# Key norms as one reciprocal per token and head, and the last two steps of a block inverse written by row ranges, in the RWKV heads of a two-block kernel

## The chip, the cores and the metric

One core of one Trainium2 chip runs the whole program: two transformer blocks over 512 tokens of width 1024. The metric is the device time of one execution in microseconds (µs); lower is better.

## The reference, cut to what matters

The change touches one stage of the second block, the RWKV-7 time mixing. For each of 16 heads of width 64, and each token, with r, k, v and the low-rank rates computed before:

```python
kk = heads(k * k_k)
kk = kk / jnp.maximum(jnp.sqrt(jnp.sum(kk * kk, axis=-1, keepdims=True)), 1e-12)
k = k * (1.0 + (a - 1.0) * k_a)
y = wkv7_scan(r_h, heads(decay), k_h, v_h, -kk, kk * a_h)
```

`kk` is divided by its own norm, which is one number per token and head. The scan is a recurrence over the tokens. The kernel does it in chunks of 128 tokens, and for each chunk and head it needs the inverse of a 128x128 unit lower triangular matrix, which it builds by doubling: blocks of 1, 2, 4, ... 64 rows, seven steps.

## The kernel before, in words

`rwkv_heads` (L1609) works on pairs of heads: 8 pairs, 128 channels each (two heads of 64) by 512 tokens (NCH = 4 chunks of 128). Each pair goes through four parts, and the loop `rwkv_turns` (L1577) runs them staggered, one turn for each pair:

- **invert** (pair i): steps s = 1 to 6 of the doubling (s = 0 is done by `grow_first`, L1798, without a product). In step s TensorE makes products of 64 columns in bf16 (`lx`, L2150), ScalarE casts them to a high part (`between`, L2003), VectorE writes the low part (`between_low`, L1813), TensorE multiplies again (`xlx`, L2168), ScalarE casts the high part into `added` (`added_high`, L2010), and VectorE writes the low part into `added` and copies both parts under a mask into the inverse X and its transpose XT (`grow`, L1821). The next step's `lx` of a head waits for that head's `grown`. Both heads go one after the other.
- **chain** (pair i-1): the recurrence over the 4 chunks in 12 parts, two in each step s, spread over TensorE, VectorE and ScalarE (L2181, L1838, L2017).
- **prepare** (pair i+1): early steps one by one in steps s = 1 to 6 (the tables `early`, L1781, L1979 and L2118), and the rest in `late`.
- **finish** (pair i-1): in `late`, at the end of a turn.

Every engine runs its own instructions strictly in the order in which the code writes them; semaphores tie the engines together (`steps.wait`, `steps.done`). So the order written in `turn` (L1921, L2074, L2241) is what decides. In step s VectorE does: `between_low`, the early step of prepare, the first part of the chain, `grow`, the second part of the chain. ScalarE does: `between`, the early step, chain, `added_high`, chain. TensorE does: `lx`, chain, `xlx`, chain, the early step.

The norm of the keys before: ScalarE squares kk in s = 2; TensorE multiplies it with a matrix of ones per head at the end of s = 3 (`norm`, L2109), which puts each norm's square on all 64 channels of its head; ScalarE takes the root of 128x512 in s = 4 (`root`, L1969), with a load of its table of functions before it; VectorE takes the maximum, the reciprocal and the product over 128x512 in s = 5 (`unit_keys`, L1753), and in s = 6 `keys_and_rates` (L1759). TensorE's step of s = 4 is `gate` (L2113), two products of 512 columns in f32 that another part of the head needs at the end of `late`; it writes bank 0 of PSUM, where the norm's product lay before.

At the end of a turn TensorE's `late` starts with the bonus product (L2122), then the transposes (L2128) and the products `grams` (L2147). VectorE's `late` starts with `columns` (L1765) and masks the grams as they come (L1789).

## Time and profile before

| | µs |
|---|---|
| median of 3 runs | 3725.72 (3723.64 to 3744.84) |
| profiled execution, its own time | 3741.53 |
| its span, from the first to the last instruction | 3739.7 |
| RWKV heads in it, from 1893 to 2568 | 675 |
| the eight turns start at | 1922.8, 1990.0, 2067.6, 2147.5, 2224.7, 2306.1, 2385.1, 2463.7 |
| TensorE busy over the span | 3078.2 (82%) |
| VectorE busy over the span | 2437.0 (65%) |
| ScalarE busy over the span | 1234.2 (33%) |

In the profile PE is TensorE (PEld its weight loads), DVE is VectorE, ACT is ScalarE. In a row of the timeline the first number is the start, in µs from the span's start, the second the duration of the piece, then engine, line, operation, written tile and read tiles, shape and count; in brackets the idle time of the engine before it and what ended it. Granted clock 1.00 is TensorE's 2.4 GHz level, 0.50 its 1.2 GHz level. The turn that starts at 2147.5 is used as the example; it is the fourth of the eight and has all four parts.

### The profile page before, as it was taken

To read this page: it belongs to the slowest core of one execution; us is meant where nothing else is said; L and a number is where in the kernel's file an instruction comes from. 1 tells how busy PE (TensorE), PEld (TensorE's weight loads), DVE (VectorE), ACT (ScalarE), POOL (GpSimd) and SP (SyncE) were. 2 spreads that over 40 slices of the span, in tenths; PEclk is the share of its full clock that TensorE was granted. 3 is DMA by queue.
4 is the path that set the end of the run, shared out by engine and by line. 5 is a ranking of instruction groups with operands and counts; after the bars stand their busy time and mean duration, and the time that the engine had idled before them with its cause. 6 is when DMAs were issued, how large, how long until landed. Compare 5 with 4: busy or idle time off the path is not lost. (4 is left out here: it accounts for less than half of the span.)

```text
span 3739.7 us, 59444 instructions
## 1 busy us (share of the span) xinstructions
PE 3078.2 (82%) x22778; PEld 1995.2 (53%) x22859; DVE 2437.0 (65%) x4209; ACT 1234.2 (33%) x1999; POOL 535.0 (14%) x365
## 2 busy tenths in 40 slices
PE   7686977459999999995967677775958998969987
PEld 4353444446766666663446566664445554434466
DVE  3893399967787877875357777764626553347742
ACT  2233132653333333333234334322114443223320
POOL 0550043013343333430000000000000000000000
PEclk9658988779999999997977777866955659979998
DMA  3003132478889898873100000002110006123230
GB/s 105 7 1 118 47 124 98 164 295 293 325 317 330 311 330 320 322 274 138 58 23 1 2 2 2 2 1 95 51 39 4 1 1 158 36 91 126 67 124 29
DMA packets 241977, 451.88 MB, mean 121 GB/s; under 512 B 15328, under 2 KB 153952, under 8 KB 240128
## 3 DMA queue, kind: packets, MB, share of 16 engines
q1 hardware_dynamic: 204928, 315.11, 24.1%
q0 software_dynamic: 36864, 134.23, 10.1%
q8 instruction: 124, 2.03, 0.2%
q14 instruction: 61, 0.50, 0.0%
HBM read 413.64 MB, written 35.65 MB: 120 GB/s over the span
## 5 line engine op out<-in xcount | busy, mean ns | idle before, releaser
L1310 PE MATMUL banks<-gated_hi,v_lo 128*128 128x384 bf16 (+2 forms) x1536 | 335.0, 273 | 0.0
L1310 PE MATMUL banks<-gated_lo,v_hi 128*128 128x384 bf16 (+2 forms) x1536 | 335.0, 273 | 0.0
L1310 PE MATMUL banks<-gated_hi,v_hi 128*128 128x384 bf16 (+2 forms) x1536 | 335.0, 273 | 0.0
L1297 PE MATMUL banks<-act_hi,u_hi 128*128 128x384 bf16 x768 | 252.2, 328 | 22.2 <-DVE u_lo L1232 22.2
L1297 PE MATMUL banks<-act_lo,u_hi 128*128 128x384 bf16 x768 | 252.2, 328 | 0.0
L1297 PE MATMUL banks<-act_hi,u_lo 128*128 128x384 bf16 x768 | 252.2, 328 | 0.0
L1143 POOL DMA_INDIRECT gathered_v<-in_v,first_tile_rows x128 | 177.9, 1390 | 499.5 <-DVE x_tokens L1246 470.5
L1138 POOL DMA_INDIRECT gathered_u<-in_u_rows,first_tile_rows x128 | 156.9, 1225 | 204.4 <-POOLq L982 146.7
L1310 PEld LDWEIGHTS banks<-gated_hi,v_hi 128*128 128x128 bf16 x1536 | 150.3, 98 | 55.4
L1246 DVE SCALAR_TENSOR_TENSOR x_tokens<-gathered_v,gathered_weights,x_tokens 128x1024 f32<-128x1024 f32 x128 | 164.2, 1283 | 10.4 <-DVE gathered_weights L1237 3.1
L1310 PEld LDWEIGHTS banks<-gated_hi,v_lo 128*128 128x128 bf16 x1536 | 139.5, 98 | 38.9
L1254 DVE CUSTOM_DVE_ANT_0 gathered_product<-gathered_u,first_tile_normed 128x1024 f32<-128x1024 f32 x128 | 155.9, 1218 | 3.3 <-DMA gathered_u<-in_u_rows,first_tile_rows 3.3
L1268 DVE TENSOR_TENSOR gated<-gelu,gate_group 128x384 f32<-128x384 f32 x96 | 53.4, 556 | 158.7 <-ACT gelu L1204 149.7
L1257 DVE TENSOR_TENSOR v_lo<-v_raw,v_hi 128x1024 bf16<-128x1024 f32 x128 | 156.1, 1220 | 0.0
L1204 ACT ACTIVATE gelu<-banks 128x384 f32<-128x384 f32 x96 | 47.1, 491 | 325.4 <-PE banks L1297 281.8
L1310 PEld LDWEIGHTS banks<-gated_lo,v_hi 128*128 128x128 bf16 x1536 | 139.5, 98 | 22.4
L1216 ACT CAST gated_hi<-gated 128x384 bf16<-128x384 f32 x128 | 65.2, 509 | 238.8 <-DVE gated L1268 227.2
L1232 DVE TENSOR_TENSOR u_lo<-u_raw,u_hi 128x1024 bf16<-128x1024 f32 x96 | 117.4, 1223 | 39.4 <-ACT u_hi L1189 39.3
L358 PE MATMUL banks<-act_lo,ffn_up_w_hi 128*128 128x512 bf16 x346 | 131.9, 381 | 12.7 <-DVE ffn_up_w_lo L317 12.4
L1196 ACT CAST v_hi<-v_raw 128x1024 bf16<-128x1024 f32 x128 | 133.4, 1043 | 0.0
L2008 ACT CAST between<-banks 128x512 bf16<-128x512 f32 (+1 forms) x96 | 52.8, 550 | 239.3 <-PE banks L2165 239.3
L358 PE MATMUL banks<-act_hi,ffn_up_w_hi 128*128 128x512 bf16 x345 | 131.3, 380 | 0.5
(608 smaller groups left out, 8281.2 us busy)
## 6 DMA issues: line engine op xcount, KB each, us to landing
v_raw<-in_v SPq DMA_DIRECT2D x128, 512.0 KB, 11.6
u_raw<-in_u SPq DMA_DIRECT2D x96, 512.0 KB, 11.7
gate_tables<-gate_piece SPq DMA_DIRECT2D x12, 2048.0 KB, 6.3
gate_group<-gate_tables SPq DMA_DIRECT2D x32, 768.0 KB, 15.8
ffn_up_raw<-in_ffn_up SPq DMA_DIRECT2D x20, 1024.0 KB, 7.3
early_u_raw<-in_u SPq DMA_DIRECT2D x32, 512.0 KB, 3.7
rwkv_in_raw<-in_w_in SPq DMA_DIRECT2D x5, 2048.0 KB, 7.9
ffn_down_raw<-in_ffn_down SPq DMA_DIRECT2D x3, 2816.0 KB, 14.5
```

The lines of the kernel that those rows point to most:

```text
L358: m = pe.matmul(bank[0:cols.stop - cols.start, :], w[:, slot, d, cols], x[:, d, :], **flags)
L1138: pool.indirect_dma_start(gu[:, n % GROUP, :], None, u_table, bass.IndirectOffsetOnAxis(ap=rows.index[:, 0, n:n + 1], axis=0)).then_inc(gu ...
L1143: pool.indirect_dma_start(gv[:, n % GROUP, :], None, v_table, bass.IndirectOffsetOnAxis(ap=rows.index[:, 1, n:n + 1], axis=0)).then_inc(gv ...
L1196: act.copy(vh[:, j, :], v_raw[:, j, :]).then_inc(v_hi, 1)
L1216: act.copy(wh[:, j, :], gh[:, j % 2, :]).then_inc(w_hi, 1)
L1232: dve.tensor_tensor(ul[:, j], u_raw[:, slot * LIVE + j], uh[:, j], ALU.subtract).then_inc(u_lo, 1)
L1246: dve.scalar_tensor_tensor(k.x[:, 0, :], gv[:, j, :], wts[:, slot, j:j + 1], k.x[:, 0, :], ALU.mult, ALU.add).then_inc(added, 1)
L1254: dve.tensor_tensor_reduce(prod[:], gu[:, j, :], rows.first[:], 1.0, 0.0, ALU.mult, ALU.add, dots[:, slot, j:j + 1]).then_inc(dotted, 1)
L1257: dve.tensor_tensor(vl[:, j, :], v_raw[:, j, :], vh[:, j, :], ALU.subtract).then_inc(v_lo, 1)
L1268: dve.tensor_tensor(gh[:, j % 2, :].rearrange("p (c t) -> p c t", t=TCH), src.rearrange("p (c t) -> p c t", t=TCH), gate[:, slot, :, j, :] ...
L1297: m = pe.matmul(ps[:, SCORE_BANK + (slot + j) % 2, 0:DT], u[:, j, d, :], x[:, d, P:], start=(d == 0 and n == 0), stop=(d == KD - 1 and n = ...
L1310: m = pe.matmul(ps[:, bank, to:to + width], v[:, j, cols], w[:, j, tok:tok + width], start=start and n == 0 and to == 0, stop=stop and n = ...
```

## The change

Two edits in the same function.

1. **Norms.** The square sums are made as 128 tokens x 2 heads for each chunk (kk squared is the stationary operand, two columns of the ones matrix the moving one), 8 numbers per partition in place of 512. Root, maximum and reciprocal work on 128x8. ScalarE then copies the reciprocals to 128x512 (`wide_norms`), and TensorE turns them back to channels with four products with the identity (`spread_norm`); VectorE multiplies kk with the bank. The steps move: maximum and reciprocal to s = 4, ahead of `key_rate`; the wide copy to s = 5, ahead of the decays; the spreading product to the end of s = 5; the product with kk to s = 6; and `gate` on TensorE from the end of s = 4 to the end of s = 6, since it waits for `unit`.
2. **Rows.** For s = 5 and 6 (blocks of 32 and 64 rows) `added` and the masked copies go. ScalarE casts the high part, and VectorE subtracts for the low part, straight into the row ranges of X and XT: in s = 5 four pieces of 32 partitions x 128 for each head and engine, in s = 6 one of 64 partitions x 256.

```diff
+BY_ROWS = 5
...
+        def rows_grown(slot, s, h):
+            b = 1 << s
+            for w, buf in ((0, X[:]), (1, XT2[slot])):
+                if s == STAGES - 1 and w == 0:
+                    continue
+                for n in range(HALF // b):
+                    first = (2 * n + 1 - w) * b
+                    rows = slice(first, first + b)
...
+                    yield bank, hi, lo
...
                 def unit_keys(j):
+                    steps.wait("prepare", "tensor", j, "spread")
+                    done(dve.tensor_tensor(kk, kk, ps[:, 0, :], ALU.mult), "unit", hold=True)
+
+                def inverse_norms(j):
                     steps.wait("prepare", "scalar", j, "root")
                     done(dve.tensor_scalar(nrm[:], nrm[:], 1e-12, None, ALU.max), hold=True)
-                    done(dve.reciprocal(nrm[:], nrm[:]), hold=True)
-                    done(dve.tensor_tensor(kk, kk, nrm[:], ALU.mult), hold=True)
+                    done(dve.reciprocal(nrm[:], nrm[:]), "inverse")
...
-                early = {1: square_root_argument, 3: decay_sums, 4: key_rate, 5: unit_keys, 6: keys_and_rates}
+                early = {1: square_root_argument, 3: decay_sums, 4: norms_and_rate, 6: keys_over_norms}
...
+                def grow_rows(i, slot, s):
+                    for h in range(2):
+                        steps.wait("invert", "scalar", i, f"added{s}{h}")
+                        for bank, hi, lo in rows_grown(slot, s, h):
+                            ins = dve.tensor_tensor(lo, bank, hi, ALU.subtract)
+                        steps.done("invert", ins, f"grown{s}{h}")
...
-                    done(act.activation(nrm[:], ps[:, 0, :], ACT.Sqrt), "root")
+                    done(act.activation(nrm[:], ps[:, 0, 0:2 * NCH], ACT.Sqrt), "root")
+
+                def wide_norms(j):
+                    steps.wait("prepare", "vector", j, "inverse")
+                    done(act.copy(nrm_wide[:].rearrange("p (n e) -> p n e", e=HD),
+                                  nrm[:].unsqueeze(2).to_broadcast([P, 2 * NCH, HD])), "wide")
...
-                early = {1: weights, 2: decay_in, 3: rate, 4: root, 5: decays}
+                early = {1: weights, 2: decay_in, 3: rate, 4: root, 5: norms_and_decays}
...
+                        if s >= BY_ROWS:
+                            for bank, hi, lo in rows_grown(slot, s, h):
+                                ins = act.copy(hi, bank)
+                            steps.done("invert", ins, f"added{s}{h}")
+                            continue
...
-                    done(pe.matmul(ps[:, 0, :], ones_h[:], kk2, start=True, stop=True), "norm")
+                    for c in range(NCH):
+                        ins = pe.matmul(ps[:, 0, 2 * c:2 * c + 2], kk2[:, c * P:(c + 1) * P], ones_h[:, 0:P:HD],
+                                        start=True, stop=True)
+                    done(ins, "norm")
+
+                def spread_norm(j):
+
+                    steps.wait("prepare", "scalar", j, "wide")
+                    for c in range(NCH):
+                        ins = pe.matmul(ps[:, 0, c * P:(c + 1) * P], nrm_wide[:, c * P:(c + 1) * P], k.ident[:],
+                                        start=True, stop=True)
+                    done(ins, "spread")
 
                 def gate(j):
-                    steps.wait("prepare", "scalar", j, "root")
+                    steps.wait("prepare", "vector", j, "unit")
                     pe.matmul(ps[:, 0, :], wj[:, 1, :], z[:, 25, :], start=True, stop=False)
                     done(pe.matmul(ps[:, 0, :], wj[0:32, 2, :], z[0:32, 26, :], start=False, stop=True), "gate")
 
-                early = {1: decay_in, 2: rate_in, 3: norm, 4: gate}
+                early = {1: decay_in, 2: rate_in, 3: norm, 5: spread_norm, 6: gate}
```

On TensorE, in the kernel before, step s = 4 of a full turn ends with the two gate products (L2115, L2116), between the chain's u product (L2202) and `lx` of step 5 (L2165):

```order
L2178 MATMUL banks<-between,inv 128x64 x12
L1574 REGISTER_ALU
L2202 MATMUL banks<-rhs,inv_t 128x64 x6
L1574 REGISTER_ALU
L2115 MATMUL banks<-z_columns,low_rank_w 128x512
L2116 MATMUL banks<-z_columns,low_rank_w 128x512
L1574 REGISTER_ALU
L2165 MATMUL banks<-inv,low_t 128x64 x12
```

In the changed kernel (its line numbers) the same two products (L2182, L2183) stand at the end of step s = 6, behind the last part of the chain (L2281 to L2283) and ahead of the bonus product (L2189) and the transposes (L2195):

```order
L2281 MATMUL banks<-state,r_dec 128x64
L2282 MATMUL banks<-u_tokens,grams_t 128x64
L2283 MATMUL banks<-bkv_tokens,grams_t 128x64
L1580 ISA
L2182 MATMUL banks<-z_columns,low_rank_w 128x512
L2183 MATMUL banks<-z_columns,low_rank_w 128x512
L1580 REGISTER_ALU
L2189 MATMUL banks<-rk,head_ones 128x512
L1580 REGISTER_ALU
L2195 MATMUL banks<-ident,b_dec 128x128 x4
```

So the gate has moved past two steps of the inverse and past six parts of the chain.

On VectorE, in the kernel before, step s = 5 of a full turn, from the norm (L1755 to L1757) to the first head's growth of the inverse (L1827):

```order
L1755 TENSOR_SCALAR kk_norm<-kk_norm 128x512
L1569 REGISTER_ALU
L1756 RECIPROCAL kk_norm<-kk_norm 128x512
L1569 REGISTER_ALU
L1757 TENSOR_TENSOR act_hi<-act_hi,kk_norm 128x512
L1569 REGISTER_ALU
L1574 REGISTER_ALU
L1851 TENSOR_TENSOR state_sum<-banks,state 128x64
L1569 REGISTER_ALU
L1852 TENSOR_SCALAR state<-state_sum,state_factors 128x64
L1574 REGISTER_ALU
L1827 TENSOR_TENSOR added<-banks,added 128x2x256
```

In the changed kernel step s = 5 has the state (L1893, L1894) at once and then the row ranges of both heads (L1858):

```order
L1850 TENSOR_TENSOR between<-banks,between 128x512
L1580 REGISTER_ALU
L1893 TENSOR_TENSOR state_sum<-banks,state 128x64
L1575 REGISTER_ALU
L1894 TENSOR_SCALAR state<-state_sum,state_factors 128x64
L1580 REGISTER_ALU
L1858 TENSOR_TENSOR inv<-banks,inv 32x4x32 x2
L1858 TENSOR_TENSOR x_tokens<-banks,x_tokens 32x4x32 x2
L1580 REGISTER_ALU
L1858 TENSOR_TENSOR inv<-banks,inv 32x4x32 x2
L1858 TENSOR_TENSOR x_tokens<-banks,x_tokens 32x4x32 x2
```

And in step s = 4 of the changed kernel the maximum and the reciprocal (L1780, L1781), which wait for ScalarE's root, stand ahead of the key rate (L1768 to L1771), and so ahead of the chain's right side (L1889, L1890), which follows:

```order
L1780 TENSOR_SCALAR kk_norm<-kk_norm 128x8
L1575 REGISTER_ALU
L1781 RECIPROCAL kk_norm<-kk_norm 128x8
L1580 REGISTER_ALU
L1768 ISA
L1768 TENSOR_SCALAR act_hi<-act_hi,cols,one_less 128x512
L1575 REGISTER_ALU
L1770 TENSOR_TENSOR act_hi<-act_hi,z_columns 128x512
L1575 REGISTER_ALU
L1771 ISA
L1771 SCALAR_TENSOR_TENSOR rk<-z_columns,cols,act_hi 128x512
```

The wait for the root, which stood in step 5, now stands in step 4, with all of VectorE's work of that step behind it.

## Rows read from the trace of the kernel before

**Rows 1.** Busy time by turn: the fourth turn, and the last, which prepares nothing

```profile
core 0: us, PE busy (x) PEld busy (x) DVE busy (x) ACT busy (x) POOL busy (x), PEclk, DMA share, GB/s
2147.50:2224.70 77.20, 57.04 (x764) 46.91 (x764) 61.22 (x128) 30.50 (x62) 0.00 (x0) 0.81 0.01 2
2463.70:2534.00 70.30, 50.72 (x660) 45.66 (x660) 41.85 (x90) 16.26 (x37) 0.00 (x0) 0.60 0.00 1
```

**Rows 2.** The fourth turn in three stretches, then step s = 5; columns as above

```profile
2147.50:2161.50 14.00, 8.15 (x112) 7.00 (x112) 8.35 (x18) 3.68 (x10) 0.00 (x0) 0.64 0.01 2
2161.50:2198.50 37.00, 28.65 (x489) 22.66 (x488) 31.13 (x62) 17.19 (x30) 0.00 (x0) 1.00 0.01 2
2198.50:2212.50 14.00, 12.47 (x91) 10.14 (x92) 10.36 (x23) 5.22 (x15) 0.00 (x0) 0.51 0.01 2
...
2188.20:2198.60 10.40, 6.88 (x125) 6.06 (x124) 9.19 (x15) 5.08 (x8) 0.00 (x0) 1.00 0.01 2
```

**Rows 3.** Timeline of the fourth turn, step s = 4 and the start of s = 5

```profile
2182.52 1.28 ACT L1971 ACT_TABLE_LOAD   x1
...
2183.15 0.54 DVE L1747 TENSOR_SCALAR act_hi<-act_hi,cols,one_less 128x512 f32<-128x512 f32 x1
...
2183.82 0.60 ACT L1971 ACTIVATE kk_norm<-banks 128x512 f32<-128x512 f32 x1
...
2185.26 0.28 DVE L1847 CAST rhs<-banks 128x128 bf16<-128x128 f32 x1
...
2185.93 0.35 PE L2202 MATMUL banks<-rhs,inv_t 128*128 128x64 bf16 x6 [1.19 <-DVE rhs L1848]
...
2186.11 1.10 PE L2115 MATMUL banks<-z_columns,low_rank_w 128*128 128x512 f32 x2
...
2188.20 0.52 PE L2165 MATMUL banks<-inv,low_t 128*128 128x64 bf16 x12
...
2189.79 0.52 PE L2165 MATMUL banks<-inv,low_t 128*128 128x64 bf16 x12 [0.72 <-DVE x_tokens L1834]
```

**Rows 4.** Timeline of the fourth turn, step s = 5 and the start of s = 6

```profile
2191.31 1.28 ACT L1975 ACT_TABLE_LOAD   x1
...
2192.38 3.35 DVE L1756 RECIPROCAL kk_norm<-kk_norm 128x512 f32<-128x512 f32 x1
...
2194.18 1.05 ACT L2015 CAST added<-banks 128x512 bf16<-128x512 f32 x2
...
2196.58 0.23 DVE L1851 TENSOR_TENSOR state_sum<-banks,state 128x64 f32<-128x64 f32 x1
...
2197.01 0.68 DVE L1827 TENSOR_TENSOR added<-banks,added 128x512 bf16<-128x512 f32 x1
2197.15 0.29 PEld L2195 LDWEIGHTS banks<-state,a_dec 64*128 64x128 f32 x2 [2.92 <-DVE state L1852]
...
2199.09 0.82 PE L2165 MATMUL banks<-x_tokens,low 128*128 128x64 bf16 x12 [0.41 <-DVE x_tokens L1834]
```

**Rows 5.** Timeline of the fourth turn, from the second head of s = 6 to the grams

```profile
2200.88 0.28 DVE L1847 CAST rhs<-banks 128x128 bf16<-128x128 f32 x1
...
2201.02 0.82 PE L2165 MATMUL banks<-x_tokens,low 128*128 128x64 bf16 x12 [1.11 <-DVE x_tokens L1834]
...
2206.70 2.02 PE L2122 MATMUL banks<-rk,head_ones 128*128 128x512 f32 x2
...
2208.51 1.06 PE L2128 MATMUL banks<-ident,b_dec 128*128 128x128 f32 x4
...
2212.89 0.73 DVE L1789 COPY_PREDICATED grams_t<-tri_masks,banks 128x512 f32<-128x512 uint32 x1 [3.12 <-issue]
```

**Rows 6.** Groups over the RWKV heads: prices of short VectorE and ScalarE operations

```profile
L1848 DVE TENSOR_TENSOR rhs<-banks,rhs 128x128 bf16<-128x128 f32 x31 | 9.0, 291 | 1.1
L1875 DVE RECIPROCAL gn_stats<-gn_stats 128x8 f32<-128x8 f32 x7 | 1.4, 195 | 0.3 <-ACT gn_stats L2041 0.3
L1950 ACT COPY low_rank_w<-decay_rate_w 128x128 f32 x6 | 1.8, 301 | 0.0
```

More of the change, by code:

```diff
@@ L1520, in rwkv_names, with held @@
     lows = [f"low{m}{h}" for m in range(2) for h in range(2)]
+    def held(s):
+        return ["-"] if s < BY_ROWS else []
     return {
         "prepare": {
-            "vector": ["kk", "-", "-", "sums", "-", "-", "rk", "-", "-", "-", "-", "-", "turnable", "-", "columns"]
+            "vector": ["kk", "-", "-", "sums", "-", "inverse", "-", "-", "rk", "unit", "-", "-", "turnable", "-", "columns"]
                       + grams[:4] + ["-"] + grams[4:] + ["bonus"] + ["-"] * 4,
-            "scalar": ["wj", "v", "decay_in", "kk2", "rate", "root", "-", "-", "decays", "-", "factors", "tok0", "tok1", "tok2",
+            "scalar": ["wj", "v", "decay_in", "kk2", "rate", "root", "wide", "-", "-", "decays", "-", "factors", "tok0", "tok1", "tok2",
                        *lows, "gate"],
-            "tensor": ["decay_in", "rate_in", "norm", "gate", "bonus", "turned0", "turned1", "turned2"] + grams + lows,
+            "tensor": ["decay_in", "rate_in", "norm", "spread", "gate", "bonus", "turned0", "turned1", "turned2"] + grams + lows,
         },
         "invert": {
-            "vector": ["-", "-", "-", "grown0"] + [n for s in stages for n in (f"between{s}0", f"between{s}1", "-", f"grown{s}0",
-                                                                         "-", f"grown{s}1")],
+            "vector": ["-", "-", "-", "grown0"] + [n for s in stages for n in (f"between{s}0", f"between{s}1", *held(s), f"grown{s}0",
+                                                                         *held(s), f"grown{s}1")],
             "scalar": [f"{n}{s}{h}" for s in stages for n in ("between", "added") for h in range(2)],
@@ L1638, in rwkv_heads @@
         x_room = k.x[:].rearrange("p t d -> p (t d)")
-        nrm = sb("kk_norm", [P, S])
+        nrm = sb("kk_norm", [P, 2 * NCH])
+        nrm_wide = sb("kk_norm_wide", [P, S])
         rk = sb("rk", [P, S])
@@ L1683, in view_blocks @@
             return buf.rearrange("p m (n two b) -> p m n two b", two=2, b=b)[:, :, :, odd, :]
+        def rows_grown(slot, s, h):
[6 more added lines that the diff above has]
+                    rows = slice(first, first + b)
+                    bank = ps[rows, 4 + h, :].rearrange("p (w m n b) -> p w m n b", w=2, m=NCH, b=b)[:, w, :, n, :]
+                    hi, lo = (buf[rows, h, l].rearrange("p m (n two b) -> p m n two b", two=2, b=b)[:, :, n, w, :]
+                              for l in range(2))
+                    yield bank, hi, lo
         def passes(left, right):
@@ L1819, in between_low @@
                                    f"between{s}{h}")
+                def grow_rows(i, slot, s):
[4 more added lines that the diff above has]
+                        steps.done("invert", ins, f"grown{s}{h}")
                 def grow(i, slot, s):
+                    if s >= BY_ROWS:
+                        return grow_rows(i, slot, s)
                     b = 1 << s
@@ L2084, in turn @@
                         if invert:
-                            added_high(i, s)
+                            added_high(i, slot, s)
                         if chained:
```

14 lines of the change are left out of this document (12 added, 2 removed).

## The prediction

> **What bounds the kernel now.** I read the busy time by turn first. The change lives in the RWKV heads, 675 µs of a span of 3739.7, and in them a full turn takes about 79 µs, of which TensorE is busy 57 and VectorE 61 [rows 1]. Neither is full, so the two take turns in waiting: a ring TensorE, ScalarE, VectorE, TensorE through each step of the inverse. Next the same turn in stretches [rows 2]. The granted clock is 1.00 from 2161.5 to 2198.5, through steps s = 2 to 5, and 0.51 from 2198.5 to 2212.5, just where TensorE is fullest (12.47 of 14.00). So TensorE runs its densest stretch at the 1.2 GHz level.
>
> Then the timeline of step 5 [rows 4] says why. VectorE holds everything: reciprocal from 2192.38 for 3.35, the state update only at 2196.58, growth of the inverse at 2197.01. TensorE waits 2.9 for the state and again for the inverse. It had been mostly idle for 4 µs when the clock fell. From 2201.02 on it has no wait worth naming until the grams; there VectorE waits 3.12 for it [rows 5]. So: VectorE bounds steps 4 and 5, TensorE bounds from step 6's second head to the grams. An edit is worth what it does to the bound of its own stretch. A program that differs by less than 1% (37 µs) is about what a measurement here can't tell from no change; over six full turns that is 6 µs a turn.
>
> All steps below are for the turn at 2147.5, as shifts against it.
>
> **Step 4, which gets longer.** VectorE now needs the root here. It is free at 2183.15; ScalarE's table load ends at 2183.80 [rows 3], and a root of 8 columns should take about 0.2 (the row of 128x8 on VectorE has 0.195 [rows 6]; both ends 0.15 to 0.3). So the root is there at 2184.0 and VectorE waits 0.9. Then maximum and reciprocal, 2 x 0.195 and a small gap: 0.45. Key rate, the chain's right side and the growth stand behind it, so all are +1.35. TensorE's u product, at 2185.93 behind VectorE's right side, comes at 2187.3.
> The gate leaves here: 2 x 1.10, from 2186.11 to 2188.2 [rows 3]. It was under cover: step 5's first product started at 2188.20 right behind it, and the second head's, at 2189.79, waited for VectorE 0.72. Both heads' growth comes 1.9 apart on VectorE, so the first was ready some 0.3 before its start: the gate's going gives that for one head and nothing for the other. First head +1.0, second +1.35.
>
> The Trainium skill (ScalarE: Activation LUTs, What ACT_TABLE_LOAD costs) says that a table switch takes about 2.66 µs, the load of 1.28 and a drain behind it of 1.38. If so, the root would come 1.4 later still and each full turn would lose that much more, some 8 µs in all. The trace does not agree: the load at 2182.52 ends at 2183.80 and the root starts at 2183.82 [rows 3]. I go by the trace.
>
> **Step 5, which gets shorter.** VectorE loses maximum, reciprocal and product, 2191.9 to 2196.58, 4.65 [rows 4]. What is late next? ScalarE. Its table load starts at 2191.31 and its first cast of `added` at 2194.18, 2.9 later, with the three exponentials between. Shifted by 1.35, and with the wide copy ahead (128x512, by the root's row 0.60 [rows 3]), the first cast starts at 2196.1. Then four pieces of 128 columns: 0.301 each alone [rows 6]; two casts of 512 take 1.05 where one takes 0.59, so neighbours overlap by about 0.1, and four take 0.9. VectorE's four pieces, 0.291 each [rows 6], with the same overlap take 0.95 behind it, the second head's another 0.95. Growth of both heads ends at 2198.9, where before it ended at 2200.88 [rows 5]. Gain 2.0 while TensorE is at its upper level. The row ranges bring 3.87 down to 1.9 of VectorE time; ScalarE pays 0.7 of it back.
>
> The Trainium skill (VectorE: DVE Perf Modes, The TRN2 errata) speaks against this edit: each instruction pays a fixed cost, so tile by 512 elements or more. Its figures would give a ScalarE cast of 128 columns from PSUM (172 + 128) / 1.2, an estimate of 0.25 without overlap, eight of them 2.0 against my 1.7: 0.3 more in a turn, 2 µs in all. The fixed part is in the trace too (128 columns cost 0.291, not a quarter of 0.68), but 0.95 for four pieces replaces 3.87 / 2 for a subtraction of 0.68 and two masked copies, so the edit still gains.
>
> The spreading product: 4 products of 128 columns, as many columns as one of 512, 1.1 at the upper level and 2.0 at the lower [rows 3, 5]. Bounds 0.5 (if short ones run like the transposes, 1.06 for four at the lower level [rows 5]) and 2.6. I take 1.0 and 1.9. In the upper case TensorE waits for the inverse anyway and it is hidden. The norm product in step 3 shrinks and was hidden.
>
> **The clock in steps 4 and 5.** TensorE finishes step 4's second multiplication at 2184.74 (1.19 idle before 2185.93 [rows 3]), then has the u product (0.35) at 2187.3 and nothing until 2189.2, since the gate that stood in this hole is gone. That hole is as empty as the one that let the clock fall before. I expect it to fall here, near 2191, and to return as it did before, 14 µs after [rows 2], near 2205. Then step 5 is bound by TensorE. A dozen products of 64 columns take 0.82 in place of 0.52 [rows 3, 4], 1.58 times as long. TensorE was busy 6.9 of step 5 at the upper level (the last of [rows 2]); that is 10.9 at the lower, and 1.9 for the spreading product makes 13, from 2189.2 on with small holes at the start. Step 6's first product starts near 2203, where it was 2199.09.
>
> **Step 6 and late.** From here on I take the upper level. The second head's first product of step 6 starts near 2204.6. From that point to the bonus product it took 5.7 at the lower level (2201.02 to 2206.70 [rows 5]); divided by 1.58 that is 3.6, to 2208.2. VectorE has added the product with kk, 0.7, and saved 1.4 in growth by rows, both beside TensorE's work: nothing. **The gate now stands on the path**: 2 x 1.10 to 2210.3 or so, bonus 1.1 to 2211.4, transposes start there, 2208.51 before [rows 5]: +2.9. Twelve transposes at 1.06 for four with some overlap take 2.7 at the lower level and half at the upper, 1.3 back, and the first grams, which began just before the clock's return, some 0.3. So +1.3 in each full turn; what follows (masks, the finish) hangs on the grams and moves along.
>
> **Sum.** Six full turns 6 x 1.3 = 7.8. The first two preparations (ahead of the loop, and in the first turn, without a chain) run at the lower level mostly: the gate, 4.0 there, becomes exposed, and what VectorE saves, about 1.4, goes off: 2.6 each, 5.2. The last full inverse (last turn, clock 0.60, and TensorE-bound): 0.5 gained by rows. +12.5. The profiled execution took 3741.53, 16 above the median of 3725.72; the sum is made on it, and I put the difference on the median: 3738, about 0.3% more.
>
> **Rivals.**
> *The clock stays up.* If the holes of step 4 don't drop it and step 5's hole is gone, step 6's second product starts at 2199.1 (2.0 before 2201.02), and the transposes at 2199.1 + 3.6 + 2.2 + 1.1 = 2206.0: -2.5, and -4.1 with what the transposes and grams give back. 6 x -4.1 + 4.7 = -20: 3706. For it: the reciprocal's hole, which let it fall before, is gone. Against: the new hole a step earlier. Chance 0.20.
> *The clock falls where it did before*, behind step 5 (holes in step 4 a little shorter than I think). Step 5 gains 2.0; then 2199.1 + 5.7 + 4.0, and the return near 2210 cuts the bonus to 1.5: transposes at 2210.3, +1.8, less 1.6 given back, +0.2. 6 x 0.2 + 4.7 = 6: 3732. Chance 0.22.
> *Slower.* The clock falls in step 4 and does not return before the gate, because step 5 still has holes. Then from 2204.6 there are 5.7 to the gate, 4.0 for it and 1.8 to the transposes, all at the lower level: 2216.1, 7.6 later than before. 6 x 7.6 + 4.7 = 50: 3776. It decides when the lower level lasts over 20 µs, as it does at the head of a turn, where TensorE has long holes. For it: the first rows of the turn stand at 0.64 [rows 2]. Against: at the lower level TensorE is full from 2192 on. Chance 0.10.
> The forecast has 0.43; 0.05 is left for what I don't see.
>
> **How the numbers follow.** The cases lie at 3706, 3732, 3738 and 3776; the runs before spread from 3724 to 3745. The range 3702 to 3762 holds the first three with some 6 µs for their sizes (root 0.15 to 0.3, spreading 0.5 to 2.6) and leaves out the slow one. Faster by over 1% (under 3688) would need the first rival doubled: 0.06. Slower by over 1% (over 3763): the slow rival, 0.09. Within 1%: 0.85.
>
> **What would show it.** Right: VectorE waits about 0.9 for the root in step 4 of each full turn; reciprocals of 0.2; TensorE's u product of step 4 starts 1.3 later after `lx` 4; the gate's two products run without a gap between the chain's last product and the bonus; the lower level begins in step 5, not 6. Wrong: a granted clock of 1.00 from step 2 to the grams (then the first rival), no wait for the root, or grams that come earlier in the turn than before.

## The result, and the profile after

| | kernel before | changed kernel |
|---|---|---|
| median (4 runs each) | 3724.68 (3719.05 to 3744.84) | 3755.94 (3753.77 to 3757.01) |
| ratio, 95% interval | | 1.0076 (1.0043 to 1.0109) |
| profiled execution, its own time | 3741.53 | 3755.15 |
| span | 3739.7 | 3753.4 |
| the same, measured more often | 3743.5 (26 runs, 3722.75 to 3759.53) | 3752.03 (10 runs, 3737.79 to 3758.82) |
| ratio of those | | 1.0028 (1.0008 to 1.0048) |

The change makes no difference above 1%. Four runs of a kernel can mislead here: before spreads over 37 µs in 26 runs, and three of its first four lay at the fast end, so the first two medians are 31 apart. Measured more often, the change costs 0.28%, some 10 µs. The forecast was +12.5.

The page of the changed kernel, the parts on busy time and on the granted clock in 40 slices (of about 94 µs each; the RWKV heads are slices 21 to 28):

```profile
span 3753.4 us, 59680 instructions
...
PE 3112.2 (83%) x22890; PEld 2032.0 (54%) x22971; DVE 2387.5 (64%) x4177; ACT 1243.4 (33%) x2055; POOL 533.9 (14%) x365
...
PEclk9658988679999999997977777776965559979998
```

VectorE lost 49.5 µs of work, TensorE gained 34.0. Of TensorE's gain 14.4 is the new spreading product; most of the rest is the same work at a lower clock, as the next rows show. The heads and their parts in the changed kernel: from the first memset to the next normalization (this ends some 9 µs behind the 2568 of the table of before), the six full turns, the end behind the last inverse, and the attention stage of the same block, whose code the change doesn't touch:

```profile
core 0: us, PE busy (x) PEld busy (x) DVE busy (x) ACT busy (x) POOL busy (x), PEclk, DMA share, GB/s
1896.30:2581.30 685.00, 519.71 (x6224) 437.65 (x6224) 443.26 (x986) 254.77 (x552) 5.49 (x4) 0.71 0.02 8
1998.40:2473.80 475.40, 378.48 (x4668) 322.78 (x4668) 330.74 (x740) 192.80 (x416) 0.00 (x0) 0.73 0.01 2
2473.80:2581.30 107.50, 73.84 (x792) 63.87 (x792) 48.33 (x109) 20.53 (x56) 0.00 (x0) 0.61 0.06 20
2822.60:3092.50 269.90, 255.86 (x1664) 156.15 (x1665) 149.86 (x441) 125.31 (x384) 0.00 (x0) 0.53 0.00 1
```

The same four stretches of the kernel before:

```profile
1892.40:2577.40 685.00, 494.67 (x6112) 403.87 (x6112) 493.07 (x1018) 245.23 (x496) 5.49 (x4) 0.73 0.02 8
1991.40:2465.20 473.80, 349.77 (x4584) 287.11 (x4584) 367.72 (x763) 185.42 (x374) 0.00 (x0) 0.78 0.01 2
2465.20:2577.40 112.20, 79.21 (x792) 68.69 (x792) 51.16 (x113) 19.67 (x50) 0.00 (x0) 0.56 0.05 20
2817.30:3082.50 265.20, 248.93 (x1664) 152.04 (x1665) 149.53 (x441) 125.28 (x385) 0.00 (x0) 0.55 0.00 1
```

VectorE is busy 49.8 µs less in the heads (443.26 for 493.07), and the stage took 685.0 in both. The granted clock of the six full turns fell from 0.78 to 0.73, and TensorE's busy time rose by 28.7 with only two per cent more instructions, of which the spreading product is 11.2; the norm products take 6.42 for 6.46 before. The spans differ by 13.7, but not in this stage: the attention stage is 4.7 longer (TensorE busy 6.9 more with the same 1664 instructions at a lower clock), the rest is spread before and behind it. One trace each is too little for a difference of 10 µs; the experiments below carry it.

Inside the fourth turn, which starts at 2158.0 now (2147.5 before, so 10.5 is to be taken off to compare), the turn as a whole (counted from 2159.4, 1.4 behind its first copy, to the same place of the next), then four stretches of it, which answer to [rows 1, 2]:

```profile
2159.40:2238.10 78.70, 63.60 (x778) 54.11 (x778) 55.14 (x124) 31.74 (x69) 0.00 (x0) 0.74 0.01 1
2189.10:2199.30 10.20, 8.69 (x112) 7.68 (x111) 7.80 (x18) 3.82 (x7) 0.00 (x0) 0.50 0.01 2
2199.30:2202.80 3.50, 1.07 (x30) 0.95 (x31) 3.44 (x8) 0.89 (x3) 0.00 (x0) 0.99 0.02 5
2202.80:2216.40 13.60, 13.60 (x140) 12.42 (x137) 4.72 (x15) 6.79 (x16) 0.00 (x0) 0.50 0.01 1
2216.40:2230.10 13.70, 12.02 (x109) 9.08 (x110) 11.49 (x29) 5.48 (x15) 0.00 (x0) 1.00 0.00 1
```

Between step 2 and the grams the clock is at the 1.2 GHz level twice, for 10.2 and 13.6 µs, where before it was there once for 14. Four of the six full turns go this way; in the other two the lower level lasts through from the first fall, for 20 and 27 µs. In the second stretch TensorE is busy every moment of it (13.60 of 13.60): there it is the bound, and VectorE, freed of its work, is busy for 4.72.

The timeline of the same turn, steps s = 3 to 6, which answers to [rows 3, 4, 5]:

```profile
2188.28 1.06 PE L2168 MATMUL banks<-head_ones,act_lo 128*128 128x2 f32 x8
...
2193.98 1.28 ACT L2013 ACT_TABLE_LOAD   x1
2195.27 0.18 ACT L2013 ACTIVATE kk_norm<-banks 128x8 f32<-128x8 f32 x1
2195.48 0.17 DVE L1780 TENSOR_SCALAR kk_norm<-kk_norm 128x8 f32<-128x8 f32 x1 [0.80 <-ACT kk_norm L2013]
...
2198.74 0.50 PE L2269 MATMUL banks<-rhs,inv_t 128*128 128x64 bf16 x6 [0.38 <-DVE rhs L1890]
2200.67 0.53 PE L2232 MATMUL banks<-inv,low_t 128*128 128x64 bf16 x12 [1.43 <-DVE x_tokens L1876]
...
2209.25 0.53 ACT L2067 CAST inv<-banks 32x128 bf16<-32x128 f32 x2 [1.15 <-PE banks L2245]
2209.78 0.52 ACT L2067 CAST x_tokens<-banks 32x128 bf16<-32x128 f32 x2
2210.34 0.59 DVE L1858 TENSOR_TENSOR inv<-banks,inv 32x128 bf16<-32x128 f32 x2 [4.59 <-ACT x_tokens L2067]
2210.95 0.58 DVE L1858 TENSOR_TENSOR x_tokens<-banks,x_tokens 32x128 bf16<-32x128 f32 x2
2212.75 2.02 PE L2176 MATMUL banks<-ident,kk_norm_wide 128*128 128x128 f32 x8
2214.56 1.49 PE L2232 MATMUL banks<-x_tokens,low 128*128 128x64 bf16 x24
...
2219.23 1.08 PE L2182 MATMUL banks<-z_columns,low_rank_w 128*128 128x512 f32 x2
...
2221.29 1.13 PE L2189 MATMUL banks<-rk,head_ones 128*128 128x512 f32 x2
2222.26 0.60 PE L2195 MATMUL banks<-ident,b_dec 128*128 128x128 f32 x4
2224.86 0.72 DVE L1821 COPY_PREDICATED grams_t<-tri_masks,banks 128x512 f32<-128x512 uint32 x1 [1.82 <-issue]
```

The norm product that stood before in the place of L2168, in the trace of before:

```profile
2177.41 1.08 PE L2111 MATMUL banks<-act_lo,head_ones 128*128 128x512 f32 x2
```

Three readings. The clock falls at 2189.1, 0.8 after the first of the eight short norm products (L2168) starts; before it stayed up for 21 µs from that place on. In step 5 VectorE waits 4.59 for ScalarE, which had waited for TensorE: the bound has changed sides. And the gate (L2182) stands between the last chain product and the bonus (L2189) with no gap on either side.

### The profile page after: what moved, and what is told of

Its sections match the earlier page's. It is cut to its first block and busy times, and to the rows that moved or that the text cites. A ratio compares the mean times of both kernels' runs of the same rounds, so it can differ in the third digit from the quotient of the medians.

```text
span 3753.4 us, 59680 instructions
## 1 busy us (share of the span) xinstructions
PE 3112.2 (83%) x22890; PEld 2032.0 (54%) x22971; DVE 2387.5 (64%) x4177; ACT 1243.4 (33%) x2055; POOL 533.9 (14%) x365
## 5 line engine op out<-in xcount | busy, mean ns | idle before, releaser
L2232 PE MATMUL banks<-inv,low_t 128*128 128x64 bf16 x960 | 56.6, 223 | 101.2 <-DVE x_tokens L1842 31.2
```

Source lines behind the costliest of these rows:

```text
L2232: ins = pe.matmul(out, one, other, start=n == 0, stop=n == 2)
```

## The experiments

Twelve kernels; the ratio is to the kernel before, run beside each on the same chip, with its 95% interval. Its median there was 3743.5 for before_same, after_same and the two halves, 3740.2 (31 runs) for rows_gate_six, gate_late, inverse_in_five and both_moves, 3742.79 (22) for gate_twice and the two with gate_four, and 3740.32 (11) for norm_filled. The stage is the 685.0 of above; "six" is the mean length of the six full turns; the clock is theirs. "Fall" is where the clock first falls after 18 µs of each of these turns, counted from the second pair of copies at its head (L1809 before). Stage, six, clock and fall are from one profiled execution each, and two of the same kernel differ by up to 10 µs in the stage.

| kernel | median (runs) | ratio | stage | six | clock | fall |
|---|---|---|---|---|---|---|
| before | 3743.5 (26) | | 685.0 | 79.0 | 0.78 | 50 to 52 |
| before_same | 3739.76 (10) | 0.9990 (0.9964 to 1.0017) | 675.4 | 78.5 | 0.78 | 36 to 50 |
| after_same | 3752.03 (10) | 1.0028 (1.0008 to 1.0048) | 692.2 | 79.8 | 0.72 | 29 to 30 |
| norms_only | 3757.63 (10) | 1.0034 (1.0014 to 1.0053) | 691.4 | 80.0 | 0.74 | 29 to 32 |
| rows_only | 3703.84 (5) | 0.9902 (0.9872 to 0.9932) | 663.9 | 76.3 | 0.81 | 36 to 51 |
| rows_gate_six | 3752.67 (10) | 1.0029 (1.0005 to 1.0053) | 692.2 | 80.9 | 0.73 | 41 |
| gate_twice | 3748.29 (10) | 1.0008 (0.9982 to 1.0034) | 687.3 | 79.4 | 0.79 | 41 to 51 |
| gate_late | 3747.56 (10) | 1.0006 (0.9985 to 1.0028) | 682.2 | 79.8 | 0.74 | 30 to 31 |
| inverse_in_five | 3728.71 (10) | 0.9977 (0.9956 to 0.9998) | 671.3 | 76.3 | 0.78 | 29 to 32 |
| both_moves | 3726.63 (10) | 0.9966 (0.9949 to 0.9984) | 663.7 | 75.6 | 0.79 | 29 to 39 |
| gate_four | 3715.21 (10) | 0.9941 (0.9914 to 0.9967) | 654.6 | 75.3 | 0.81 | 29 to 33 |
| gate_four_inverse_five | 3705.38 (7) | 0.9906 (0.9879 to 0.9933) | 647.4 | 73.8 | 0.82 | 29 to 39 |
| norm_filled | 3703.54 (6) | 0.9900 (0.9876 to 0.9925) | 643.3 | 72.5 | 0.87 | 67 to 70 |

**The two kernels again**, unchanged:

> The kernel before, once more, for a second trace of it and its own spread. In the first traces the RWKV stage took 685.0 us in both kernels, from the first ones of the scan to the next normalization, and the difference of 13.7 us lies outside it; the medians differ by 31. Theory A (the first trace of before was taken in one of its long executions, and the stage does cost time): this trace takes 3720 to 3730 and its RWKV stage is 10 us or more shorter than 685. Theory B (the stage is equal, and the time is lost in other stages, whose instructions are the same, by where the clock's changes fall in them): the stage takes 683 to 687 again, and the stages outside it are shorter than in the first trace by some 15 us.

> The changed kernel once more, for a second trace. Its runs lay between 3753.8 and 3757.0. Theory A: RWKV stage 685 again, and the other stages as in the second trace of before. Theory B: RWKV stage within 3 us of 685, other stages longer than in before by 10 to 30 us.

Before against itself is 0.9990, not to be told from 1. The change comes out at 1.0028. In this pair of traces a full turn grows from 78.5 to 79.8, by 1.3, where the first pair has 0.3; the stage grows by 16.8, where the first pair has nothing. Neither theory came out as written: the stage of before did come out 10 shorter, but in an execution of 3739.28, and that of the changed kernel came out 7 longer.

**Each half alone.** norms_only turns the second edit off:

```diff
-BY_ROWS = 5
+BY_ROWS = STAGES
```

rows_only is the kernel before with the second edit. Against the changed kernel its tables of steps differ as follows, and the functions of the norm and the gate are those of before too:

```diff
-                early = {1: square_root_argument, 3: decay_sums, 4: norms_and_rate, 6: keys_over_norms}
+                early = {1: square_root_argument, 3: decay_sums, 4: key_rate, 5: unit_keys, 6: keys_and_rates}
-                early = {1: weights, 2: decay_in, 3: rate, 4: root, 5: norms_and_decays}
+                early = {1: weights, 2: decay_in, 3: rate, 4: root, 5: decays}
-                early = {1: decay_in, 2: rate_in, 3: norm, 5: spread_norm, 6: gate}
+                early = {1: decay_in, 2: rate_in, 3: norm, 4: gate}
```

> The norms' edit alone; the last two steps of the inverse with added and masked copies as before. If the moved gate and the root's wait are the loss, this is slower than before by more than the whole change: growth in steps 5 and 6 takes 1.9 more on VectorE in each of six full turns, so +5 to +12 us on the changed kernel, 3760 to 3768. If the rows are the loss (short pieces on ScalarE and VectorE), this is 3725 to 3740.

> The row ranges alone; norms and gate as before. If the norms' edit is the loss: 3700 to 3722, since VectorE, which is the bound in step 5 behind the reciprocal, gives back 1.9 in each of six full turns and TensorE's hole before step 6 shrinks, with the root, the gate and the wide copy where they were. If the rows are the loss: over 3735.

The rows edit alone is worth 1.0%, the norms edit alone costs 0.34% (3757.63, a little under the 3760 to 3768 expected), and both together cost 0.28%. So the halves don't add: on top of the norms edit the rows edit is worth 0.06%, within the noise. The reason is in the stretches above: with the norms edit TensorE bounds step 5, and VectorE's savings there release nothing. The trace of norms_only agrees. Its stretch that answers to the third one has TensorE full too, and VectorE, with all its masked copies, is busy for less than half of it:

```profile
2202.00:2215.70 13.70, 13.70 (x140) 12.52 (x140) 6.30 (x15) 5.92 (x11) 0.00 (x0) 0.50 0.01 1
```

The six full turns of rows_only (its 3.35 µs reciprocal of [rows 4] still in step 5), to be set beside those of before and after:

```profile
1991.90:2449.60 457.70, 342.02 (x4584) 282.56 (x4584) 351.43 (x738) 191.86 (x410) 0.00 (x0) 0.81 0.01 2
```

**The gate's place.** rows_gate_six is rows_only with the gate moved from s = 4 to s = 6 and nothing else; gate_twice adds the gate's two products in s = 4 again, for nothing, to fill the hole (s = 6 writes over them).

```diff
-                early = {1: decay_in, 2: rate_in, 3: norm, 4: gate}
+                early = {1: decay_in, 2: rate_in, 3: norm, 6: gate}
```
```diff
-                early = {1: decay_in, 2: rate_in, 3: norm, 6: gate}
+                early = {1: decay_in, 2: rate_in, 3: norm, 4: gate_twice, 6: gate}
```

> The row ranges as in rows_only, with the norms of before, and the gate's two products alone moved from the end of step 4 to the end of step 6. Theory G (the gate's place is the loss: in step 4 it lay beside VectorE's work and kept TensorE's clock up, in step 6 it is exposed): most of the gap between rows_only (0.990 of before) and the changed kernel (1.003) opens here, ratio 0.997 to 1.003. The six full turns average 78 to 79 us in place of 76.3, and their clock falls from 0.81 to about 0.75. Theory R (the wait for the root in step 4 is the loss): ratio within 0.003 of rows_only, clock 0.81.

> rows_gate_six with the gate's two products made a second time, at their old place at the end of step 4; the copy of step 4 is overwritten by the one of step 6, so it is work for nothing. It tells the two ways apart in which the gate's move costs. Theory E (exposure: 2.2 us at the upper level stand ahead of the bonus in step 6): as slow as rows_gate_six or slower, RWKV stage 690 to 700. Theory C (the clock: without these products TensorE has a hole in step 4 and runs steps 3 to 6 at the lower level): the clock over the six full turns rises from 0.73 to about 0.80 and the stage comes down from 692 to 677 to 683, with only the exposed 2.2 a turn left over the 664 of rows_only.

Moving the gate alone costs 1.3% (0.9902 to 1.0029), all that the rows edit gave and more; a full turn takes 80.9 where 78 to 79 had been expected. Three stretches of the fourth turn (30 to 41, 41 to 50 and 50 to 68 µs into it, counted as the fall is) in rows_only:

```profile
2174.70:2185.70 11.00, 8.17 (x128) 5.47 (x127) 10.02 (x23) 4.35 (x8) 0.00 (x0) 0.97 0.01 1
2185.70:2194.70 9.00, 6.22 (x110) 5.59 (x107) 7.26 (x10) 6.18 (x14) 0.00 (x0) 0.85 0.01 2
2194.70:2212.70 18.00, 16.42 (x140) 13.78 (x140) 13.90 (x39) 6.17 (x16) 0.00 (x0) 0.71 0.01 1
```

The same stretches in rows_gate_six:

```profile
2191.00:2202.00 11.00, 6.45 (x136) 5.10 (x134) 10.02 (x22) 4.44 (x9) 0.00 (x0) 1.00 0.01 1
2202.00:2211.00 9.00, 8.07 (x93) 7.39 (x93) 7.16 (x10) 5.12 (x11) 0.00 (x0) 0.50 0.01 2
2211.00:2229.00 18.00, 18.00 (x96) 12.60 (x97) 8.88 (x22) 5.82 (x19) 0.00 (x0) 0.50 0.01 1
```

And in gate_twice:

```profile
2180.80:2191.80 11.00, 8.16 (x120) 5.45 (x120) 10.02 (x23) 4.35 (x8) 0.00 (x0) 1.00 0.01 1
2191.80:2200.80 9.00, 6.91 (x117) 6.11 (x116) 7.39 (x9) 6.18 (x14) 0.00 (x0) 0.81 0.01 2
2200.80:2218.80 18.00, 17.33 (x95) 12.03 (x96) 9.52 (x24) 4.62 (x14) 0.00 (x0) 0.54 0.00 1
```

In the first row TensorE's busy time falls from 8.17 to 6.45 when the gate leaves; the clock then falls at its end, in every full turn at 41, and stays at the 1.2 GHz level until 68 in four of the six turns, this one among them, where TensorE is full to the end, and until 51 in two. The copy in s = 4 restores 8.16 and most of the clock of the first two stretches (0.79 over the full turns in place of 0.73), but the lower level still covers the end of the turn (0.54), and the stage gets only 5 µs back of 28, where 9 to 15 had been expected from the clock. The interval of gate_twice overlaps that of rows_gate_six, so the clock's share alone isn't settled. That most of the cost stays when the hole is filled speaks for the gate's exposed place at the end of the turn, but this is argued: its two products are 13 µs over six turns at the upper level, and no run takes them wholly off the path with the hole left open (gate_late, below, comes nearest).

**Root and gate within the changed kernel.** inverse_in_five moves maximum and reciprocal from s = 4 to s = 5 (and the wide copy behind the decays); gate_late moves the gate behind the grams; both_moves does both.

```diff
-                early = {1: square_root_argument, 3: decay_sums, 4: norms_and_rate, 6: keys_over_norms}
+                early = {1: square_root_argument, 3: decay_sums, 4: key_rate, 5: inverse_norms, 6: keys_over_norms}
...
-                    wide_norms(j)
                     decays(j)
+                    wide_norms(j)
```
```diff
-                early = {1: decay_in, 2: rate_in, 3: norm, 5: spread_norm, 6: gate}
+                early = {1: decay_in, 2: rate_in, 3: norm, 5: spread_norm}
...
                         grams(j, slot, 0, 6)
+                        gate(j)
```

> The changed kernel, with maximum and reciprocal of the norms back at the head of step 5 on VectorE, where the root is long there, and the wide copy on ScalarE behind the decays. Takes away the 0.80 wait for the root and 0.45 of work in step 4. Theory R: ratio to before 0.990 to 0.996, turns near 77. Theory G: at most 1.3 us in each of six turns, ratio 1.000 to 1.003.

> The changed kernel, with the gate's products moved on from the end of step 6 into late, behind the sixth group of gram products and ahead of the turning of y, where TensorE waits 1.6 us for VectorE in each full turn. Theory G, its exposed half: 2.2 us a turn are taken off the path before the grams and 0.6 added behind, so six times 1.6, some 10 us less than the changed kernel, ratio 0.998 to 1.001. If the loss is only the clock in steps 3 to 5: no change from the changed kernel, 1.003.

> inverse_in_five and gate_late together. If both terms are real and add up: the changed kernel less 8 and less 10 us, ratio 0.996 to 1.000. Under 0.990 it would beat the row ranges alone; that would need the norms' edit to gain 4.2 us of VectorE time in step 5, which I expect only if step 5 is bound by VectorE there.

Taking the root's wait out of s = 4 gives 0.5% (1.0028 to 0.9977): a full turn goes from 79.8 to 76.3, up to 3.5, more than the 1.3 of the wait and its work. The clock went up with it, 0.72 to 0.78. This lies between the two theories (0.990 to 0.996, and 1.000 to 1.003). What went is the second fall: 55 µs into the turn the changed kernel is at the lower level in 11 of the 12 full turns of its two traces, gate_late in 6 of 6, inverse_in_five in none. The gate behind the grams gives 0.2%, with overlapping intervals. It is exposed in another place, ahead of the finish: in the fourth turn VectorE waits 0.83 for the product behind it, for which it waited nothing in the changed kernel. Both together (0.9966) aren't told apart from inverse_in_five.

**The gate back under its cover.** gate_four keeps the norms edit but lets the gate run in s = 4: the spread product writes bank 1, so the gate need no longer wait for the product with kk.

```diff
-                    done(dve.tensor_tensor(kk, kk, ps[:, 0, :], ALU.mult), "unit", hold=True)
+                    done(dve.tensor_tensor(kk, kk, ps[:, 1, :], ALU.mult), "unit", hold=True)
...
-                        ins = pe.matmul(ps[:, 0, c * P:(c + 1) * P], nrm_wide[:, c * P:(c + 1) * P], k.ident[:],
+                        ins = pe.matmul(ps[:, 1, c * P:(c + 1) * P], nrm_wide[:, c * P:(c + 1) * P], k.ident[:],
...
-                    steps.wait("prepare", "vector", j, "unit")
+                    steps.wait("prepare", "scalar", j, "root")
...
-                early = {1: decay_in, 2: rate_in, 3: norm, 5: spread_norm, 6: gate}
+                early = {1: decay_in, 2: rate_in, 3: norm, 4: gate, 5: spread_norm}
```

(The bonus product, which writes bank 1 too, waits for `unit` in its place.) gate_four_inverse_five adds the first diff of the group above.

> The whole change, with the gate left at the end of step 4 as before; so that bank 0 can hold it, the spreading product goes to bank 1, which the chain's state has left by then, and the bonus product waits until VectorE has used it. If the gate's move is the main loss, this is close to rows_only: stage 663 to 675, ratio to before 0.989 to 0.996; what is left over rows_only is the wait for the root, 1.25 a turn. If the norms' edit loses by itself: stage over 680.

> gate_four with maximum and reciprocal at the head of step 5 and the wide copy behind the decays. No wait for the root, no moved gate, 4.2 us less of VectorE in step 5: it should beat rows_only, which has the long reciprocal: stage 650 to 662, ratio 0.984 to 0.990. If it only equals rows_only, ScalarE (table load, three exponentials and the wide copy ahead of the casts of step 5) has become the bound of step 5 in VectorE's place.

0.9941 against 1.0028: the gate's place costs the changed kernel 0.9%, and the stage fell further than expected (654.6, for 663 to 675). Here too the second fall is gone in five turns of six, though the root's wait is still in s = 4. So, with the norms edit in, the second stretch at the lower level came only where the gate was gone from s = 4 and the root's wait stood there; either move took it away but for that one turn. With the inverse in s = 5 as well it is 0.9906 (the two intervals overlap), 1.2% below the changed kernel, though TensorE executes the same work. In the heads:

```profile
1896.10:2550.80 654.70, 487.08 (x6224) 404.12 (x6224) 443.09 (x987) 255.69 (x552) 5.51 (x4) 0.77 0.02 8
...
2792.90:3042.50 249.60, 230.56 (x1664) 142.03 (x1665) 148.80 (x441) 125.18 (x384) 0.00 (x0) 0.60 0.00 1
```

The first row is the stage in gate_four: 30.3 shorter than the 685.0 of the changed kernel at the same instruction counts. The second is the attention stage: 249.6 against 265.2 and 269.9, with TensorE's 1664 instructions taking 230.56, 248.93 and 255.86. Nothing in it was edited. It is a source of noise of the size of the effect, and why the stage is the better measure for an edit in the heads.

gate_four_inverse_five was expected to beat rows_only, having 4.2 µs less of VectorE in step 5. By its ratio it only equals it (0.9906 and 0.9902); the stage is 16.5 shorter, but that is one trace of each, and the one of rows_only is its slowest execution of five. The traces show why step 5 gives so little. The fourth turn starts at 2144.7 in both; growth by rows in its step 5 starts at 2193.88 in gate_four_inverse_five, and in rows_only, behind the long reciprocal, at 2194.61:

```profile
2193.88 0.59 DVE L1854 TENSOR_TENSOR inv<-banks,inv 32x128 bf16<-32x128 f32 x2 [3.15 <-ACT x_tokens L2063]
```
```profile
2194.61 0.60 DVE L1846 TENSOR_TENSOR inv<-banks,inv 32x128 bf16<-32x128 f32 x2
```

VectorE now waits 3.15 for ScalarE, which runs the table load, three exponentials, the wide copy and the casts without a break from 2189.29 to 2194.93. ScalarE has become the bound of step 5: of the 4.2 saved on VectorE, 3.15 goes into this wait.

**The short norm products.** In the seven kernels that have the short norm products alone (eight traces, 48 full turns) the clock falls some 30 µs into the turn: it is at the upper level when the first of them starts, and falls 0.65 to 1.4 µs later in 44 turns, 2.8 to 3.9 in the other four. With the old product in their place (30 full turns of five traces) no fall came sooner than 6 µs after its start. norm_filled is gate_four_inverse_five with one product of 512 columns ahead of them, whose result they write over: work added for nothing.

```diff
                     steps.wait("prepare", "scalar", j, "rate")
+                    pe.matmul(ps[:, 0, :], ones_h[:], kk2, start=True, stop=True)
                     for c in range(NCH):
```

> gate_four_inverse_five with the norm's old product of 512 columns made once more ahead of the four short ones in step 3, and overwritten by them: work for nothing, 1.1 us at the upper level, beside VectorE's growth. In every trace with the short norm products the clock fell some 30 us into most full turns, right behind them, and for 10 us or more; in those with the old product it did not fall before 35 us. Theory C (the short products let the clock fall): the fall near 30 goes, the clock over the six full turns is over 0.83 in place of 0.816, turns 72 to 73.5, ratio to before 0.984 to 0.990. Rival (the fall comes from the holes of step 4, or saves nothing since VectorE is the bound there): the clock falls as before or the stage stays at 647 to 655, ratio 0.990 to 0.994.

The same stretches (30 to 41, 41 to 50, 50 to 68) of the fourth turn in gate_four_inverse_five:

```profile
2174.70:2185.70 11.00, 9.95 (x118) 8.56 (x117) 9.06 (x19) 4.03 (x8) 0.00 (x0) 0.53 0.01 1
2185.70:2194.70 9.00, 9.00 (x135) 7.25 (x134) 4.82 (x14) 6.45 (x15) 0.00 (x0) 1.00 0.01 2
2194.70:2212.70 18.00, 14.42 (x165) 12.27 (x164) 17.32 (x43) 8.73 (x22) 0.00 (x0) 1.00 0.01 2
```

And in norm_filled, with its six full turns ahead of them:

```profile
1993.00:2427.90 434.90, 327.64 (x4680) 270.81 (x4680) 329.33 (x739) 193.59 (x416) 0.00 (x0) 0.87 0.01 2
...
2167.20:2178.20 11.00, 8.79 (x129) 6.59 (x128) 10.02 (x23) 4.13 (x8) 0.00 (x0) 1.00 0.01 1
2178.20:2187.20 9.00, 8.14 (x133) 6.95 (x132) 4.79 (x14) 6.63 (x15) 0.00 (x0) 1.00 0.01 2
2187.20:2205.20 18.00, 14.38 (x164) 12.26 (x164) 17.33 (x43) 8.72 (x22) 0.00 (x0) 1.00 0.01 2
```

The fall at 30 is gone; the clock stays up until 67 or later in all six turns. So the fall hangs on what TensorE has ahead of it there. The time hardly moves (0.9906 to 0.9900, intervals overlapping; 1.4 a turn, 4 in the stage by one trace). The rows say why. Only the first has another clock, and in it VectorE gets through 10.02 of work in place of 9.06, about 1 µs a turn. In the last the clock is up in both, and VectorE is busy 17.32 and 17.33 of 18.00, TensorE 14.4: the end of the turn is VectorE's there.

## Why the prediction came out as it did

The forecast was 3738, the medians are 3755.94 (4 runs) and 3752.03 (10), inside the range; the forecast difference of +12.5 stands against 0.0028 x 3743.5 = 10.5 (31 by the medians of four). The path of the fourth turn was forecast well from step 5 on; that the total came so close owes something to luck, as the points on the clock and on the sum show. Point by point:

- **The root's wait in step 4**: forecast 0.9 a turn and 0.45 of work behind it. Measured 0.80 (7.7 over eight turns, the longest 2.2); the root starts 0.01 behind its table load and takes 0.18, maximum and reciprocal 0.17 and 0.20. Right. The Trainium skill (ScalarE: Activation LUTs, What ACT_TABLE_LOAD costs) counts a drain behind the load; the trace does not agree here either, 2195.26 to 2195.27. But removing the wait was worth up to 3.5 a turn, since the clock moved too. The u product, forecast at 2187.3, came at 2188.2 in before's time, 0.9 later than forecast, because TensorE ran step 4 at the lower level.
- **Growth by rows**: forecast 0.95 for VectorE's four pieces, with an overlap of 0.1 between neighbours. Measured 1.17, two pieces 0.59 and the next two 0.58: no overlap. Mis-sized by 0.22 a head (the prediction's own prices, four of 0.291 less three overlaps of 0.1, make 0.86 and not 0.95). ScalarE's four took 1.05 for 0.9: one took 0.257 and not 0.301, and they don't overlap either. The Trainium skill (VectorE: DVE Perf Modes, The TRN2 errata) holds that each instruction pays a fixed cost; the trace agrees, 0.29 for each 128 columns against 0.68 for 512. It cost nothing in the changed kernel: both heads' growth ended at 2212.8, and TensorE, with the spreading product ahead, came to step 6 at 2214.56.
- **The spreading product**: 1.9 forecast at the lower level, 2.02 measured. Right.
- **The clock**: forecast to fall near 2191 in before's time, behind step 4's second product, for the hole that the gate left. It fell at 2189.1, which is 2178.6 in before's time: 12 µs earlier, behind the short norm products of step 3. The prediction wrote of the norm product that it "shrinks and was hidden". Hidden it was, as a duration, but the clock stayed up behind it as it was, and falls behind it as it is now; norm_filled, with the old product back ahead of the short ones, has no fall there. After 3.5 at the upper level the clock fell again at 2202.8, before's 2192.3: this second fall is the one forecast (2191), 13.6 long (14), with the return at before's 2205.9 (2205). The forecast laid it to the gate's hole alone; it needs the root's wait beside it, as inverse_in_five and gate_four show. The first fall is what the prediction missed. TensorE then ran step 4 at the lower level, which cost the path about 1 at the start of step 5 (before's 2190.2 for 2189.2), and by the transposes 0.4 was left of that. That 10 µs at the lower level, which stood in no term, left so little is luck.
- **Step 5 bound by TensorE, step 6 from 2203**: measured 2214.56, before's 2204.1. Right by its mechanism.
- **The gate exposed in step 6**: two products from 2219.23 to 2221.3, forecast 2208.2 to 2210.3, measured 2208.7 to 2210.8. Transposes forecast 2211.4, measured 2211.8. The first gram mask starts at 2224.86, before's 2214.4: +1.5, forecast +1.3. gate_four shows what this place costs in all: 0.9%, some 30 µs, more than the 2.2 a turn of the two products (13 in six turns); with the gate in s = 4 the clock over the full turns is 0.81, not 0.73.
- **The sum**: full turns +7.8 forecast; +1.6 in the first pair of traces (473.8 to 475.4), +8 in the second (471.0 to 479.0). First preparations +5.2 forecast, +3.1 in the first pair (ahead of the loop 1.5, first turn 1.6), +6.3 in the second. End -0.5 forecast, -4.7 (at a clock of 0.61 in place of 0.56) and +2.5. In all the stage moved by 0.0 and by +16.8, for 12.5 forecast, and in the first pair the whole 13.7 of the spans lay outside it. Two pairs of traces are too few to check the terms; the total has its 10.5 from the repeated runs alone.
- **The rivals**: "the clock stays up" fell, since the clock goes down twice between step 2 and the grams; norm_filled has such a clock, 1.00 from 18 µs on to 67 or later, but with the gate back in s = 4 and the inverse in s = 5. It is 37 below before, where the rival, with its exposed gate, was priced at 20 below; that the two medians lie close (3706 and 3703.5) says nothing, since before's was 3725.72 there and 3740.32 here. "Falls where it did before" fell as well. The slower rival did not occur in the changed kernel, but rows_gate_six comes near it: in four of its six full turns the lower level lasts from 41 to 68, through the gate and beyond.
- **The signs**: the wait, the reciprocals and the gate without a gap came as written. The u product came 1.9 later after `lx` 4 and not 1.3, and the lower level began in step 3 and not in step 5.

What stays open: how much of the 1.0% of rows_only arises in the stage. Its profiled execution gives 11 to 21 µs of 40 by its median, and the attention stage moves by more than 20 between kernels that don't touch it. How much of the gate's 0.9% is its exposure and how much the clock stays open too, and so does why the clock stays up behind one product of 512 columns and not behind eight of 2.

## What to carry to other kernels

A change that saves work on one engine may lose by what it moves on another: look up each moved instruction's cover, since a gate of 2.2 µs lay hidden under a wait and cost 0.9% on the path. Ask which engine is the next bound: of 4.2 µs saved on VectorE 3.15 went into a wait for ScalarE. Before shrinking a hidden product on TensorE, ask what keeps its clock up behind it; and test halves of a change alone, as one of these was worth 1% and the other hid it. When a program has stages whose time follows the clock, compare the stage and take ten runs before believing half a per cent.

## What was not expected of the hardware

- Eight short matmuls of 2 columns (busy 1.06 µs) fill as much time in the profile as the old product of 512 columns (1.08, two instructions). Yet the granted clock fell to the 1.2 GHz level 0.65 to 3.9 µs after the first of them started in all 48 full turns of the seven kernels that have them alone (eight traces), and near them in none of norm_filled's six, where a 512-column product stands ahead of them.
- Two VectorE subtractions of 32 partitions x 128 in a row take 0.59, twice one of 0.29: neighbours of this kind don't overlap, and neither do ScalarE's casts of that shape (0.53 for two at 0.257), though ScalarE's 512-column casts do (1.05 for two at 0.59).
- The attention stage, with the same instructions in each, took 249.6 to 269.9 µs at clocks of 0.60 to 0.53.
